# Two of sixteen experts fixed instead of three, three shared steps instead of two, in a mixture-of-experts decoder layer

## The reference, cut to what matters

```python
def _moe(u, w_rg, b_rg, w_re, b_re, w_g, w_u, w_d):
    xf = u.reshape(bsz * t, d)
    p_group = jax.nn.softmax((xf @ w_rg + b_rg).astype(F32), axis=-1)
    g_sel = jnp.argmax(p_group, axis=-1)
    ...
    top_w, top_i = lax.top_k(p_e, TOP_K_IN_GROUP)
    ...
    h = jax.nn.silu(jnp.einsum('nd,edf->nef', xf, w_g)) * jnp.einsum('nd,edf->nef', xf, w_u)
    out = jnp.einsum('nef,efd->nd', h * gates[..., None], w_d)
```

## Time and profile before

| | us |
|---|---|
| median of 3 runs | 550.91 (549.88, 550.91, 560.49) |
| profiled execution | 548.19 |
| its span, first to last instruction | 546.4 |
| experts on TensorE, first to last matmul of a step | 361.4 to 525.9 |
| TensorE busy | 522.6 (96% of the span) |

### The profile page before, as it was taken

One profiled execution on the slowest core, in us unless ns is written; L12 is line 12 of the kernel. 1 busy time (PEld: TensorE's weight loads), 2 busy tenths in 40 slices (PEclk: granted clock), 3 DMA queues, 4 the chain that ended last, 5 costly groups with the idle time before them and its releaser, 6 DMA issues.

```text
span 546.4 us, 7549 instructions
## 1 busy us (share of the span) xinstructions
PE 522.6 (96%) x2798; PEld 324.0 (59%) x2798; DVE 260.2 (48%) x759; ACT 151.2 (28%) x293; POOL 155.2 (28%) x166
## 2 busy tenths in 40 slices
PE   8999999999999999999999999788999999899994
PEld 6677755544455554557444445476777767477841
DVE  3444375433033142244453365684676556643347
ACT  7332597701123222232132334400001010000132
POOL 3017000116000000001210021247667757747500
PEclk8999999999999999999999999999899999989998
DMA  9999997899700000009820035879999999999684
GB/s 276 356 331 353 345 334 309 303 387 355 282 0 1 0 0 1 1 6 400 308 78 38 38 116 189 298 278 381 364 343 310 355 375 349 368 362 366 89 208 176
DMA packets 47417, 128.85 MB, mean 236 GB/s; under 512 B 5506, under 2 KB 18210, under 8 KB 41234
## 3 DMA queue, kind: packets, MB, share of 16 engines
q1 hardware_dynamic: 30912, 99.36, 49.5%
q0 software_dynamic: 11408, 24.39, 17.2%
q10 hardware_dynamic: 5058, 4.58, 2.5%
HBM read 116.48 MB, written 17.30 MB: 245 GB/s over the span
## 4 chain that ended last, share of the span: by engine, by line
PE 73%; DVE 9%; DMA 8%; issue 5%; POOL 3%; SPq 1%; ACT 0%; ACTq 0%; POOLq 0%; DVEq 0%
PE psum L810 72%; DMA arena<-gates_dram,slot_tok 4%; DMA ring<-in_w_mod_dram 2%; POOL arena L753 2%; PE psum L813 2%; DMA u_dram<-arena 2%; DVE arena L2378 1%; DVE arena L2443 1%; DVE x L2383 1%; DVE arena L2324 1%; POOL f_dram L782 0%; DVE arena L2178 0%; SPq L574 0%; DVE arena L2318 0%; DVE arena L2334 0%
## 5 line engine op out<-in xcount | busy, mean ns | idle before, releaser
L810 PE MATMUL psum<-ring,uT 128*128 128x512 f32 (+1 forms) x384 | 126.5, 522 | 0.0
L810 PEld LDWEIGHTS psum<-ring,uT 128*128 128x128 f32 (+1 forms) x384 | 56.5, 172 | 60.1 <-issue 55.8
L1493 ACT ACTIVATE arena<-psum 128x512 f32<-128x512 f32 (+6 forms) x80 | 35.7, 476 | 163.8 <-PE psum L810 152.8
L810 PE MATMUL psum<-uT,ring 128*128 128x288 f32 x256 | 64.9, 410 | 0.1
L810 PEld LDWEIGHTS psum<-arena,ring 128*128 128x128 f32 x512 | 60.1, 196 | 6.8 <-issue 6.8
L810 PE MATMUL psum<-arena,ring 128*128 128x128 f32 x512 | 60.6, 280 | 3.7 <-DVE arena L2534 2.1
L753 POOL DMA_INDIRECT arena<-u_dram,part_tok x52 | 53.4, 1028 | 23.2 <-issue 14.0
L810 PEld LDWEIGHTS psum<-uT,ring 128*128 128x128 f32 x256 | 47.7, 190 | 16.4 <-issue 4.0
L810 PE MATMUL psum<-ring,arena 128*64 128x256 f32 (+2 forms) x192 | 51.9, 497 | 0.0
L782 POOL DMA_INDIRECT f_dram<-arena,add_tok x26 | 41.6, 1599 | 26.3 <-issue 15.9
L810 PE MATMUL psum<-arena 128*128 128x128 f32 (+6 forms) x253 | 42.0, 330 | 5.4 <-DVE arena L2324 3.1
(11 more groups left out here) (261 smaller groups left out, 604.7 us busy)
## 6 DMA issues: line engine op xcount, KB each, us to landing
ring<-in_w_mod_dram SPq DMA_DIRECT2D x24, 1024.0 KB, 11.3
ring<-in_w_exp_down_dram SPq DMA_DIRECT2D x12, 1024.0 KB, 13.5
ring<-in_w_exp_gate_dram SPq DMA_DIRECT2D x11, 1024.0 KB, 8.9
ring<-in_w_exp_up_dram SPq DMA_DIRECT2D x11, 1024.0 KB, 12.3
ring<-in_w_in_dram SPq DMA_DIRECT2D x10, 1024.0 KB, 10.7
ring<-in_w_out_dram SPq DMA_DIRECT2D x4, 1024.0 KB, 6.5
uT<-in_w_exp_gate_dram SPq DMA_DIRECT2D x4, 1024.0 KB, 14.6
f_dram<-in_consts_dram POOLq DMA_DIRECT2D x2, 1536.0 KB, 16.2
```

Of the source, the lines that this page charges most:

```text
L810: return nc.tensor.matmul(out, lhsT, rhs, start=first, stop=last)
L1493: return nc.scalar.activation(out, src, func, **kw).then_inc(done, 1)
```

## The change

The diff, without the lines that only move a definition:

```diff
@@ -49,9 +49,9 @@
 ABSENT = 8192.0
-FIRST = 3
+FIRST = 2
 SORTED = NE - FIRST
-STEPS = [()] * FIRST + [(0,), (1,), (9, 10), (2,), (3,), (4,), (11, 12), (5,), (6,), (7,), (8,)]
+STEPS = [()] * FIRST + [(0,), (1,), (8, 9), (2,), (3,), (10, 11), (4,), (5,), (12, 13), (6,), (7,)]
 NST = len(STEPS)
...
@@ -298,7 +298,6 @@
         rank1 = region(14336 + 3 * TILES * NE, TILES, NE)
         spare = region(14816, 1)
...
@@ -471,7 +470,7 @@
         expert_pieces = [p for p in weight_pieces() if p[0] in ("wg", "wu", "wd")]
-        early, late = expert_pieces[:SLOTS], expert_pieces[SLOTS:]
+        early, late = expert_pieces[:3 * FIRST], expert_pieces[3 * FIRST:]
         assert all(slot[p] < SLOTS for p in early)
...
@@ -493,11 +492,12 @@
         gpick = [tiny(144 + i, 1) for i in range(2)]
+        gsl = [tiny(432 + i * NE, NE) for i in range(4)]
         lastr, lastg = tiny(152, TILES), tiny(160, TILES)
...
         grid = tiny(192, SORTED, SORTED)
 
...
@@ -766,10 +766,12 @@
                     if e >= 2:
-                        pool.wait_ge(s_eoa, e - 1)
-                        pool.wait_ge(s_eod, e - 1)
+                        pool.wait_ge(s_gs[e % 2], 16 * (e // 2))
+                    if e >= 4:
+                        pool.wait_ge(s_eoa, e - 3)
+                        pool.wait_ge(s_eod, e - 3)
                     pool.indirect_dma_start(
-                        out=gsl[e % 2], out_offset=None, in_=gates_dram,
+                        out=gsl[e % 4], out_offset=None, in_=gates_dram,
                         in_offset=bass.IndirectOffsetOnAxis(ap=slot_tok[:, e:e + 1], axis=0))\
...
@@ -782,7 +784,8 @@
                             in_offset=None, compute_op=ALU.add,
-                            out_offset=bass.IndirectOffsetOnAxis(ap=add_tok[:, e:e + 1], axis=0))\
+                            out_offset=bass.IndirectOffsetOnAxis(ap=add_tok[:, e:e + 1], axis=0),
+                            bounds_check=NTOK - 1, oob_is_err=False)\
                             .then_inc(s_ost[c][e % 2], 16)
...
@@ -794,8 +797,10 @@
                             .then_inc(s_fready, 16)
-                    if 2 <= e < NST + 1:
-                        gather_gates(e - 2)
+                    if e == 2:
+                        gather_gates(0)
+                    if 2 <= e < NST:
+                        gather_gates(e - 1)
                     if e >= 3:
...
@@ -1331,8 +1336,10 @@
                     pe.wait_ge(s_xgTd, e + 2)
-                    pe.wait_ge(s_hs, e)
-                    pe.wait_ge(s_hm, FT * e)
+                    earlier = [i for i in range(e) if paired(i)]
+                    if earlier:
+                        pe.wait_ge(s_eoa, earlier[-1] + 1)
+                        pe.wait_ge(s_eod, earlier[-1] + 1)
                     for k in range(KT):
...
@@ -1342,8 +1349,8 @@
                 def pair_turn(e):
+                    pe.wait_ge(s_hm, FT * (e + 1))
                     for k in range(FT):
-                        pe.wait_ge(s_hm, FT * e + k + 1)
                         last = turn(bank[3][:, FE + k * P:FE + (k + 1) * P],
...
@@ -1365,8 +1372,9 @@
                     if e >= 1:
-                        pe.wait_ge(s_hs, e)
-                        pe.wait_ge(s_hm, FT * e)
+                        done = e - paired(e - 1)
+                        pe.wait_ge(s_hs, done)
+                        pe.wait_ge(s_hm, FT * done)
                     for w, outs in ((wg, (bank[0][:, 0:P], bank[0][:, P:FE])),
...
@@ -1837,7 +1845,7 @@
                         f(eo[e % 2][:, 0:512], bank[4], ACT.Copy, s_eoa,
-                          scale=gsl[e % 2][:, e:e + 1])
+                          scale=gsl[e % 4][:, e:e + 1])
                     elif e < NST - 1:
...
@@ -2342,8 +2350,7 @@
                     .then_inc(s_idx, 1)
-                link(v.tensor_scalar(spare, found, 0.0, con[:, C_SPARE:C_SPARE + 1],
-                                     ALU.is_equal, ALU.mult))
+                link(v.tensor_scalar(spare, found, 0.0, ABSENT, ALU.is_equal, ALU.mult))
                 v.scalar_tensor_tensor(out=add_tok[:, e:e + 1], in0=found, scalar=-1.0,
...
@@ -2450,7 +2457,7 @@
                         dve.wait_ge(s_gs[e % 2], 16 * (e // 2 + 1))
-                        v.tensor_scalar(eo[e % 2][:, 512:1024], bank[5], gsl[e % 2][:, e:e + 1],
+                        v.tensor_scalar(eo[e % 2][:, 512:1024], bank[5], gsl[e % 4][:, e:e + 1],
                                         None, ALU.mult).then_inc(s_eod, 1)
...
@@ -2497,7 +2504,7 @@
                                              float(at + 1), None, ALU.is_equal))
-                    link(v.tensor_tensor(out=masked[:, 0], in0=gsl[e % 2][:, FIRST:NE], in1=mine,
+                    link(v.tensor_tensor(out=masked[:, 0], in0=gsl[e % 4][:, FIRST:NE], in1=mine,
                                          op=ALU.mult))
...
@@ -2507,11 +2514,8 @@
                 orders()
+                take_input(0)
                 numbers(2)
-
-                take_input(0)
-                for h in range(2, NH):
-                    new_state(h)
                 gate_weights()
...
@@ -2519,6 +2523,8 @@
                 v.tensor_tensor(out=gates[:], in0=oh[0], in1=oh[1], op=ALU.add).then_inc(s_gw, 1)
+                for h in range(2, NH):
+                    new_state(h)
                 for e in range(NST):
...
```

More of the change, by code:

```diff
@@ L300, in build @@
         rank1 = region(14336 + 3 * TILES * NE, TILES, NE)
-        gsl = [region(14784 + i * NE, NE) for i in range(2)]
         spare = region(14816, 1)
@@ L498, in build @@
         grid = tiny(192, SORTED, SORTED)
-        order = tiny(368, SORTED).bitcast(I32)
-        ordf = tiny(384, SORTED)
+        order = tiny(400, SORTED).bitcast(I32)
+        ordf = tiny(416, SORTED)
         def spread(eng, parts, done):
```

## The result

| | before | after |
|---|---|---|
| median, us | 552.38 | 561.75 |
| ratio (95% interval) | 1 | 1.0188 (1.0141 to 1.0235) |
| span of the profiled execution | 546.4 | 559.3 |
| experts on TensorE, start to start of the closing matmuls | 361.4 to 525.9 | 361.0 to 537.1 |

What follows compares the result with a forecast made beforehand. TensorE was taken to bound the kernel, weight DMA a close second limit. Experts ending at 514, plus 20.5 of tail and 1 for last additions, gave 535.5 of span; with run offsets 538.5 us, 8-in-10 range 531 to 546.

Steps and rivals of the forecast that it cites:

- The work: TensorE in the experts: 14 steps become 13, 142.1 us of work instead of 152.9, so 10.8 us less.
- The front: Steps 0 and 1: 2.1 us of new wait in step 0, step 2 starting at 387.0 against 387.41, no gain.
- The first gates: Step 0's gates: done 1.4 us earlier, landing at about 378.2.
- The later gates: Gates gathered one step sooner: waits from step 3 on go, with looser pair waits also 5.2 us and most small pieces.
- The price of a full addition: GpSimd's DMA queue: an addition of 128 rows costs 1.4 us, between 1.14 and 1.9.
- The end: After the experts: waiting for the last additions adds 1 us, between 0 and 3; the tail stays at 20.5.
- From there without further loss: TensorE from step 2 to step 10: no lost time between steps, step 10 starting at 474.5.
- the sum of the weights: DMA until the 37th late piece: weights 97.3, additions 17.8, gathers 11.2, rest 6; 132.3, over 1.04 is 127.2 us.
- Wanted is it at 481.9: Step 11: its gate weights, the 37th late piece, are needed at 481.9.
- it lands at 487.7: The 37th late piece, step 11's gate weights, lands at 487.7, and step 11 starts then.
- The second rival: Weight DMA: bytes set the rate, 360 GB/s; experts end at 519, time about 543.5; chance 0.2.
- The third rival: Weight DMA: starvation outweighs the step saved, if the 37th piece lands after 500.4, 3.8 us a piece; chance 0.06.

Runs made afterwards that it cites:

- a_late: Changed kernel with VectorE's wlast block, which waits for the stored states, moved from step 2 to step 6; 551.69 us, ratio 1.001 to the kernel before.
- b_gates: Kernel before with only the gates gathered one step sooner, into four buffers; 545.71 us, ratio 0.986 to the kernel before.
- a_noadd: a_late with every slot of every addition out of bounds, so additions are issued but move nothing; 534.29 us, one run.
- a_14: a_late with 14 steps: 2 fixed, 10 single, 2 shared, six pieces loaded ahead; 551.13 us, ratio 0.998 to the kernel before.
- a_first3: a_late with three fixed experts and the 14 steps of before, nine pieces loaded ahead; 541.17 us, ratio 0.984 to the kernel before.
- a_late_nogates: a_late with the gates gathered as late as in the kernel before; 549.41 us, ratio 0.999 to the kernel before.

## Why the prediction was wrong

Right were these steps. The work: a shared step costs as much as a single one, and 10.8 us left TensorE. The front: step 2 started at 387.10 for 387.0 forecast, with a new wait of 1.98 us in step 0 for 2.1. That isn't luck: in a_late, where the matmuls behind that wait are not slow, the tokens of step 1 wait instead, and step 2 starts at 387.13. The first gates, though, came at 379.4 where I had 378.2, only 0.3 us sooner than before. The later gates: some 5 us in b_gates, though 3.9 of 5.2 at the pair, and no wait of `pick_gates` for them. The price of a full addition, 1.25 to 1.35 us more than one left out by the packets' time, 1.6 by landings, for 1.4; with it what leaving out saves. GpSimd's share from 436 to 507 us, 25.7% for 26 (the changed kernel, rows as in the earlier trace rows):

```profile
q1 hardware_dynamic: 3914, 22.07, 77.6%
q0 software_dynamic: 2886, 4.43, 25.7%
```

The end: the tail takes 22.2 instead of 20.5 us, 1.7 more for 1 forecast.

Wrong was, first, "From there without further loss", from step 2 to step 10. I had let the full queue from 359.7 on meet the weights only, and not asked which other transfer of those microseconds an engine waits for. There was one, and the view of waits of before had it with 0.88 us, too small to be looked at. Forecast 0, found 14.5 us in step 3 (11.5 of wait, the rest mostly slow matmuls behind it), and the dry queue. Net, that block costs 10 us (a_late).

Second, the sum of the weights, in two of its terms. "Wanted is it at 481.9" took the 37th piece, the gate weights, for the one that a step starts with. `expert_in` asks for both its weights before the first matmul, so it is the 38th, one interval or 3.4 us later; a_late started step 11 at 498.55, when the up weights landed (471.05 + 27.4), and its row for step 8 names the up weights. And "it lands at 487.7" took the time at which so much work is done for the time at which a piece is complete. In a_late the 26th piece landed at 427.88 + 29.6 = 457.5. The same sum gives 450.5 for it (26 x 2.63, additions of 525 rows 11.5, seven gathers 7.7, rest 6, over 1.04). The queues in a_late, first from 365 to 455 us, then SP's alone from 360.6 to 498.4:

```profile
q1 hardware_dynamic: 4834, 27.16, 74.5%
q0 software_dynamic: 3624, 5.63, 25.0%
q10 hardware_dynamic: 2080, 1.05, 3.9%
```

```profile
q1 hardware_dynamic: 7471, 42.22, 76.0%
```

27.16 MB are 25.9 pieces, and 1.1 MB, one piece more, had been moved before; so 26.9 pieces' bytes had been moved and 25 had landed. Nearly two pieces' worth, 6.5 us, lies in pieces that are not complete, and with the queue that full each one takes about 30 us from issue to landing. At 498.4 it is 40.3 pieces moved and 38 landed. I had closed the sum on the last landing of before, behind which nothing is queued, and there the two times are the same. With both terms put right the 26th piece comes out at 457.0 (measured 457.5) and the 38th at 487.7 + 3.4 + 6.5 = 497.6 (measured 498.5). The 6.5 was read at the 26th, so only the 38th is a test of it. Step 8 is starved as well as step 11, which the prediction didn't see at all. The second rival's time (543.5) was nearer, for the wrong reason: the bytes did not set the rate, the additions cost engine time (a_noadd).

The third rival, starvation that outweighs the step saved, had the sign and half of the mechanism, with a chance of 0.06. Three weights fewer ahead cost ten microseconds as starvation (a_14 against a_first3), and that alone brings the kernel back to the time of before (a_late, 1.001); it doesn't outweigh. The other ten, which make it slower, come through the stores, issued later and among more weights, and no rival named them. I put its turning point at an interval of 3.8 us from one landing to the next; in a_late it was 3.7 to the 26th piece. The 0.06 rested on "dearer traffic than any full stretch shows", which was right about the rate and said nothing of when a piece is complete.

What stays open: whether the 2.3 us that a_late_nogates seems to win over a_late are there (by the ratios it is 1.2), and why so many more bytes lie in incomplete pieces when the queue is deep.

## What to carry to other kernels

A change that takes preloading away takes its megabytes twice: they land later themselves, and they stand beside every small transfer of that moment. A transfer of small packets beside a queue of large ones that doesn't run empty advances one packet for one of theirs. Before counting on a full queue, list every wait for any DMA in the stretch, stores included, with its present slack; a wait of 0.9 us is a wait without slack, not a small one. And ask of a weight when its last byte lands, not when the sum of work reaches it.

## What the runs showed of the hardware

Two stores of 512 KB in packets of 512 bytes (2080 packets for 1.05 MB) were issued 1.2 us apart; the second, at 369.4 us with nine weights loaded ahead and at 366.2 with six, took 30.4 and 45.3 us to land. Beside a queue with weights in it they moved one packet for each packet of the weights (224 and 224 in 5 us); where that queue ran short, 1065 in 5 us.

An addition of 128 half rows (0.26 MB) into device memory costs 1.25 to 1.35 us of all sixteen engines more than one whose slots are left out, where the same bytes of weights cost 0.66, a quarter of a piece. Slots left out by the bounds check keep their packets (5536 in both kernels) but hardly cost time: gathers and twenty empty additions together took 15.2 us in a_noadd, and the prediction's 1.1 a step gives the gathers of 11.5 steps alone about 12.7 (an estimate).

With the weights' queue deep, 1.9 to 2.3 pieces' worth of bytes had been moved beyond the pieces that had landed.

Behind the waits of TensorE of 4.46 us and more that stand above with the 32 records behind them (4.46, 7.68, 5.35 and 7.25 us), these records are slow (5.2 to 6.0 us for what takes 3.8). Behind the wait of 2.0 us in step 0 they were slow in the changed kernel (5.47) and not in a_late (3.84). Stretches of the changed kernel and of a_late with the granted clock, the number before the DMA share:

```profile
366.70:370.00 3.30, 3.26 (x17) 3.26 (x18) 1.44 (x8) 0.38 (x1) 2.67 (x3) 0.57 1.00 382
```

```profile
366.90:370.00 3.10, 3.06 (x27) 3.06 (x28) 1.73 (x9) 0.38 (x1) 2.47 (x3) 1.00 0.98 378
```

At 0.57 the clock is near its lower level of 1.2 GHz; at 1.00 it is at 2.4. Which of the two follows a wait of 2 us, no run here settles.
